# First layers' key and value compression over 128 rows and one weight slot, its operand built behind the last rotation

## What is computed

```python
blk_idx = CMP_STRIDE * jnp.arange(n_cmp)[:, None] + jnp.arange(CMP_BLOCK)[None, :]

def compress(t, p, w1, w2):
    tb = t[:, :, blk_idx] + p
    hid = jax.nn.gelu(tb.reshape(B, G, n_cmp, CMP_BLOCK * Dh) @ w1)
    return hid @ w2

kc = compress(partial_rope(kv[0, 0], pos), cmp_pos[0], cmp_w1[0], cmp_w2[0])
vc = compress(kv[0, 1], cmp_pos[1], cmp_w1[1], cmp_w2[1])
s_cmp = jnp.einsum('bghsd,bgnd->bghsn', q, kc)
```

## Time and profile before

| | |
|---|---|
| median of 3 runs | 1391.33 us (1391.18 to 1391.76) |
| profiled execution | 1391.72 us, of which the span of the trace is 1389.7 us |
| instructions | 31502 |
| PE busy | 1362.7 us, 98% |
| VectorE busy | 1052.0 us, 76% |
| ScalarE busy | 843.5 us, 61% |
| GpSimd busy | 553.1 us, 40% |
| granted TensorE clock, mean | 0.999 of full speed |

### The profile page before, as it was taken

One profiled execution on the slowest core, in us unless ns is written; L12 is line 12 of the kernel. 1 busy time (PEld: TensorE's weight loads), 2 busy tenths in 40 slices (PEclk: granted clock), 3 DMA queues, 4 the chain that ended last, 5 costly groups with the idle time before them and its releaser, 6 DMA issues.

```text
span 1389.7 us, 31502 instructions
## 1 busy us (share of the span) xinstructions
PE 1362.7 (98%) x13386; PEld 1168.5 (84%) x13386; DVE 1052.0 (76%) x1395; ACT 843.5 (61%) x1349; POOL 553.1 (40%) x448
## 2 busy tenths in 40 slices
PE   8999999999999999999999999999999999999997
PEld 7778888888778888888778888888888778988887
DVE  6897886557897884568888898756978865898853
ACT  5684554337675544346896755645788888675652
POOL 0144995122056992224210576603114212366610
PEclk9999999999999999999999999999999999999999
DMA  9543466544343666535335365553643333476551
GB/s 364 185 147 128 170 211 208 198 167 152 123 142 107 239 213 206 189 107 167 122 122 212 143 224 183 176 188 119 213 152 122 100 130 126 150 245 211 194 170 32
DMA packets 37020, 234.65 MB, mean 169 GB/s; under 512 B 4752, under 2 KB 7824, under 8 KB 10384
## 3 DMA queue, kind: packets, MB, share of 16 engines
q1 hardware_dynamic: 36880, 232.63, 48.8%
HBM read 231.57 MB, written 1.05 MB: 167 GB/s over the span
## 4 chain that ended last, share of the span: by engine, by line
PE 76%; DVE 12%; ACT 7%; issue 3%; POOL 1%; DMA 1%; ACTq 0%; DVEq 0%; SPq 0%; POOLq 0%
PE psum L734 22%; PE psum L736 21%; PE psum L735 21%; DVE low L2428 4%; ACT high L1734 2%; PE psum L819 1%; PE psum L820 1%; PE psum L821 1%; ACT m L2136 1%; PE psum L944 1%; DMA raw<-stream 1%; PE psum L940 1%; POOL h L3258 1%; POOL m L3256 1%; DVE arena L2535 1%
## 5 line engine op out<-in xcount | busy, mean ns | idle before, releaser
L2428 DVE SCALAR_TENSOR_TENSOR low<-raw,high 128x2048 f16<-128x2048 f32 (+5 forms) x247 | 533.1, 2165 | 186.1 <-ACT high L1734 185.4
L734 PE MATMUL psum<-u,high 128*128 128x256 f16 (+2 forms) x2008 | 552.7, 275 | 1.3 <-ACT arena L1720 1.3
L736 PE MATMUL psum<-u,low 128*128 128x256 f16 (+2 forms) x2008 | 552.4, 275 | 0.0
L735 PE MATMUL psum<-u,high 128*128 128x256 f16 (+2 forms) x2008 | 552.4, 275 | 0.0
L1734 ACT ACTIVATE high<-raw 128x2048 f16<-128x2048 f32 (+4 forms) x248 | 418.1, 1690 | 122.3 <-PE psum L736 88.6
L734 PE MATMUL psum<-arena,high 128*128 128x256 f16 (+2 forms) x1112 | 304.7, 274 | 1.7 <-DVE arena L2962 1.4
L736 PE MATMUL psum<-arena,low 128*128 128x256 f16 (+2 forms) x1112 | 304.7, 274 | 0.0
L735 PE MATMUL psum<-arena,high 128*128 128x256 f16 (+2 forms) x1112 | 304.7, 274 | 0.0
L734 PEld LDWEIGHTS psum<-u,high 128*128 128x128 f16 x2008 | 196.5, 98 | 34.2 <-issue 5.3
L735 PEld LDWEIGHTS psum<-u,high 128*128 128x128 f16 x2008 | 196.7, 98 | 28.8 <-issue 0.7
L736 PEld LDWEIGHTS psum<-u,low 128*128 128x128 f16 x2008 | 196.6, 98 | 28.1
(11 more groups left out here) (364 smaller groups left out, 1817.7 us busy)
## 6 DMA issues: line engine op xcount, KB each, us to landing
raw<-stream SPq DMA_DIRECT2D x206, 1024.0 KB, 4.8
raw<-stream SPq DMA_DIRECT2D x8, 768.0 KB, 4.2
raw<-stream SPq DMA_DIRECT2D x5, 512.0 KB, 3.6
raw<-stream SPq DMA_DIRECT2D x2, 896.0 KB, 4.5
con<-consts SPq DMA_DIRECT2D x1, 1437.0 KB, 12.3
h<-x_t SPq DMA_DIRECT2D x2, 512.0 KB, 5.8
raw<-stream SPq DMA_DIRECT2D x2, 448.0 KB, 5.2
misc<-small SPq DMA_DIRECT2D x1, 512.0 KB, 14.5
```

What stands on the lines that cost most here:

```text
L734: pe.matmul(out, w_hi, x[0], start=start, stop=False)
L735: pe.matmul(out, w_hi, x[1], start=False, stop=False)
L736: return pe.matmul(out, w_lo, x[0], start=False, stop=stop)
L2428: tell(dve.scalar_tensor_tensor(low[:, at:at + w], raw[:, off:off + w], W_SCALE, high[:, at:at + w], ALU.mult, ALU.subtract), split_ready ...
```

## The change

- The two weight slots of the compression per layer become one, `cmp_l`, of 2048 columns. Row r of the slot holds position parity and feature: window position 2i on rows 0 to 63 and 2i + 1 on rows 64 to 127. For each i, 64 columns are for keys and 64 for values. Slots behind it move up by one.
- `compressed_hidden` becomes one block: for each of 16 i, one matmul of 120 columns with the high weights (high and low operand, each 4 x 15) and one of 60 with the low weights, on all 128 rows. Keys times value windows and the reverse are computed too and not read. Keys' hidden values now lie on rows 0 to 63 and the values' on 64 to 127, and the scaling, sum and `compressed_keys` follow that.
- On PE the block stands where `compressed_hidden(0)` stood; where `compressed_hidden(1)` stood comes `one(T_PU + 1)`, which was between `turn(2)` and `compressed_keys`.
- On VectorE the two additions of `tb` behind `rotate(0)` go, and eight (key or value, head, parity) on 64 rows come behind `rotate(2)`, ahead of `give(6)`. `tb_lo` moves behind the four copies.
- On ScalarE `tb_hi` moves behind the evacuation of T_VS, ahead of `give(7)`; `compression(0)` and one of the two further low parts on VectorE go; `evac(T_PU + 1)` moves ahead; four small copies of kc and vc become two.

```diff
-        items.append(("product", f"in1_{l}", KT, [len(t) for t in nsa_gla_pool_order()], ((CMP_AFTER, f"cmp_{l}_0"), (CMP_AFTER, f"cmp_{l}_1"))))
+        items.append(("product", f"in1_{l}", KT, [len(t) for t in nsa_gla_pool_order()], ((CMP_AFTER, f"cmp_{l}"),)))
...
-                    for j in range(CMP_BLOCK):
-                        for g in range(2):
-                            r = slice(g * HD, g * HD + HD)
-
-                            at = (w1 % SPLIT) * SLOT + j * HD
-                            pe.matmul(shaped(bank(4 + g, 32 * which, 32 * which + 2 * CMP_N, r), 2, CMP_N), high[r, at:at + HD],
-                                      tb_parts[r, :, which, j, :], start=(j == 0), stop=False)
-                            mm = pe.matmul(bank(4 + g, 32 * which, 32 * which + CMP_N, r), low[r, at:at + HD], tb_hi[r, which, j, :],
-                                           start=False, stop=(j == CMP_BLOCK - 1))
+                    for i in range(CMP_BLOCK // 2):
+                        at = (w1 % SPLIT) * SLOT + i * P
+                        pe.matmul(shaped(bank(4, 0, 8 * CMP_N), 2, 4 * CMP_N), high[:, at:at + P], tb_parts[:, :, i, :], start=(i == 0), stop=False)
+                        mm = pe.matmul(bank(4, 0, 4 * CMP_N), low[:, at:at + P], tb_hi[:, i, :], start=False, stop=(i == CMP_BLOCK // 2 - 1))
                     mm.then_inc(slot_free, 1)
...
                 turn(0)
-                compressed_hidden(0)
+                compressed_hidden()
                 scores(2)
                 values(0)
                 turn(1)
-                compressed_hidden(1)
+                one(T_PU + 1)
                 scores(3)
                 values(1)
                 turn(2)
-                one(T_PU + 1)
                 compressed_keys()
...
-                act.wait_ge(tb_ready, 2 * l + 2)
-                tell(act.activation(tb_hi, tb, ACT.Copy), tb_high)
                 evac(T_Q + 1)
                 give(6)
                 evac(T_Q + 2)
                 evac(T_VS)
+                act.wait_ge(tb_ready, 2 * l + 2)
+                tell(act.activation(tb_hi, tb, ACT.Copy), tb_high)
                 give(7)
...
-                compression(0)
                 act.wait_ge(hid_summed, l + 1)
                 tell(act.activation(hid_tanh[:, :, 0:CMP_N], hid_tanh[:, :, 0:CMP_N], ACT.Tanh, scale=GELU_ROOT), hid_ready)
+                evac(T_PU + 1)
                 copy_out(1)
                 exps(3)
                 copy_pt(2)
-                evac(T_PU + 1)
...
                 rotate(0)
                 tell.settle()
-                evac_wait(T_VC)
-                for which, src in ((0, roped[:, T_KC, :]), (1, p1[:, T_VC, :])):
-                    windows = bass.AP(src.tensor, src.offset, [list(src.ap[0]), [1, CMP_BLOCK], [CMP_STRIDE, CMP_N]])
-                    pos = par[:, PAR[f"pos{l}"] + 32 * which:PAR[f"pos{l}"] + 32 * which + 32]
-                    tell(dve.tensor_tensor(tb[:, which], windows, along(pos, CMP_N), ALU.add), tb_ready)
                 give(4)
...
-                dve.wait_ge(tb_high, l + 1)
-                tell(dve.tensor_tensor(tb_lo, tb, tb_hi, ALU.subtract), tb_split)
                 dve.wait_ge(ds_done, l + 1)
...
                 rotate(2)
+                evac_wait(T_VC)
+                for which, src in ((0, roped[:, T_KC, :]), (1, p1[:, T_VC, :])):
+                    for g in range(2):
+                        r = slice(g * HD, g * HD + HD)
+                        rows = src[r, :]
+                        for odd in range(2):
+                            windows = bass.AP(rows.tensor, rows.offset + odd, [list(rows.ap[0]), [2, CMP_BLOCK // 2], [CMP_STRIDE, CMP_N]])
+                            at = PAR[f"pos{l}"] + CMP_BLOCK * which
+                            pos = par[r, at + odd:at + CMP_BLOCK:2]
+                            to = (2 * which + g) * CMP_N
+                            ins = dve.tensor_tensor(tb[odd * HD:odd * HD + HD, :, to:to + CMP_N], windows, along(pos, CMP_N), ALU.add)
+                    tell(ins, tb_ready)
                 give(6)
                 dve.wait_ge(o_done, l + 1)
                 for q in range(4):
                     dst, src = gla_out(gmix[:, 3:6, :], q)
                     ins = dve.tensor_copy(dst, src)
                 tell(ins, o_copied)
+                dve.wait_ge(tb_high, l + 1)
+                tell(dve.tensor_tensor(tb_lo, tb, tb_hi, ALU.subtract), tb_split)
                 maxima(0)
...
                 give(8)
                 weigh(3)
-                low_part(matrices[f"cmp_{l}_0"] + SPLIT)
                 maxima(4)
-                low_part(matrices[f"cmp_{l}_1"] + SPLIT)
+                low_part(matrices[f"cmp_{l}"] + SPLIT)
                 weigh(4)
```

More of the change, by code:

```diff
@@ L455, in two_stacks @@
          ep, en, qd, kinv, kend, kend_tok, gmix) = carve([
-             (N_IN1, S), (6, S), (6, S), (2, 32, 15), (2, 16), (16,), (2, HD), (4, P), (6, P), (2, 18), (12, 16), (5, 12),
+             (N_IN1, S), (6, S), (6, S), (CMP_BLOCK // 2, 4 * CMP_N), (2, 16), (16,), (2, HD), (4, P), (6, P), (2, 18), (12, 16), (5, 12),
              (2, 2, S), (2, 512), (12, P), (2, 16), (2 * S,), (2 * S,), (2 * S,),
@@ L480, in two_stacks @@
         tb_home = p1[:, T_GQ:T_GQ + 4, :].rearrange("p a b -> p (a b)")[:, 0:960]
-        tb_parts = shaped(tb_home.bitcast(F16), 2, 2, 32, 15)
-        tb_hi, tb_lo = halves(tb_home, 2, 32, 15)
+        tb_parts = shaped(tb_home.bitcast(F16), 2, CMP_BLOCK // 2, 4 * CMP_N)
+        tb_hi, tb_lo = halves(tb_home, CMP_BLOCK // 2, 4 * CMP_N)
         m_flat = m_all.rearrange("p k t -> p (k t)")
@@ L1140, in values_to_tokens, with compressed_hidden @@
                     mm.then_inc(v_turned, 1)
[L1142 removed]
+                def compressed_hidden():
                     pe.wait_ge(o_rstd, l + 1)
[L1144 removed]
+                    w1 = matrices[f"cmp_{l}"]
                     await_slot(w1)
                     pe.wait_ge(tb_split, l + 1)
[L1147 to L1155 removed]
+                    for i in range(CMP_BLOCK // 2):
+                        at = (w1 % SPLIT) * SLOT + i * P
+                        pe.matmul(shaped(bank(4, 0, 8 * CMP_N), 2, 4 * CMP_N), high[:, at:at + P], tb_parts[:, :, i, :], start=(i == 0), stop=False)
+                        mm = pe.matmul(bank(4, 0, 4 * CMP_N), low[:, at:at + P], tb_hi[:, i, :], start=False, stop=(i == CMP_BLOCK // 2 - 1))
                     mm.then_inc(slot_free, 1)
@@ L1160, in compressed_keys @@
                     for g in range(2):
-                        r = slice(g * HD, g * HD + HD)
-                        pe.matmul(bank(4 + g, 0, CMP_N, r), small_at(0, HD, r), hid[r, 0, 0:CMP_N], start=True, stop=True)
-                        mm = pe.matmul(bank(4 + g, 64, 64 + HD, slice(0, CMP_N)), hid[r, 1, 0:CMP_N], small_at(HD, 2 * HD, r),
+                        keys, values = slice(0, HD), slice(HD, P)
+                        pe.matmul(bank(4, 0, CMP_N, slice(g * HD, g * HD + HD)), small_at(0, HD, keys), hid[keys, g, 0:CMP_N], start=True, stop=True)
+                        mm = pe.matmul(bank(5, g * HD, g * HD + HD, slice(0, CMP_N)), hid[values, g, 0:CMP_N], small_at(HD, 2 * HD, values),
                                        start=True, stop=True)
@@ L1826, in give, with compression @@
                     high_part(steps[n][0] + SPLIT)
-                def compression(which):
-                    high_part(matrices[f"cmp_{l}_{which}"] + SPLIT)
+                def compression():
+                    high_part(matrices[f"cmp_{l}"] + SPLIT)
                 base = 6 * l
@@ L1935, in first_layer @@
                 copy_pt(2)
-                evac(T_PU + 1)
                 act.wait_ge(kcvc_done, l + 1)
[L1938 to L1942, removed]
+                act.activation(kc[:, 0:CMP_N], bank(4, 0, CMP_N), ACT.Copy, scale=0.5)
+                tell(act.activation(vc[0:CMP_N], shaped(bank(5, 0, P, slice(0, CMP_N)), 2, HD), ACT.Copy, scale=0.5), kcvc_ready)
                 copy_out(2)
-                compression(1)
+                compression()
                 exps(4)
@@ L2632, in first_layer @@
                 weigh(2)
-                freed_by_pe(dve, matrices[f"cmp_{l}_1"])
+                freed_by_pe(dve, matrices[f"cmp_{l}"])
                 h15, t15 = hid[:, :, 0:CMP_N], hid_tanh[:, :, 0:CMP_N]
[L2636 to L2639, removed]
+                for which in range(2):
+                    r, at = slice(which * HD, which * HD + HD), 2 * CMP_N * which
+                    high_sums = shaped(bank(4, at, at + 2 * CMP_N, r), 2, CMP_N)
+                    ins = dve.tensor_scalar(hid[r, :, 0:CMP_N], high_sums, 1.0 / W_SCALE, None, ALU.mult)
                 tell(ins)
                 tell.settle()
[L2642 to L2645, removed]
+                for which in range(2):
+                    r, at = slice(which * HD, which * HD + HD), 4 * CMP_N + 2 * CMP_N * which
+                    low_sums = shaped(bank(4, at, at + 2 * CMP_N, r), 2, CMP_N)
```

(6 more changed lines are left out.)

## The result

The changed kernel takes **1405.97 us** (median of 4 runs, 1404.39 to 1407.47) against 1391.32 of the kernel before on the same chip, a ratio of 1.0104 (95% interval 1.0088 to 1.0120). The sign and the main term were forecast. The size was not: 1397.7 was predicted, and the range ended at 1403.0. The profiled execution took 1406.91 us, of which the span is 1405.1; before it was 1391.72 and 1389.7.

What follows compares the result with a forecast made beforehand. VectorE was taken to have no room before `scores(0)`, PE only 0.3 us less. Delay +4.7 and gain −1.5 per layer made +6.4 over two: 1391.72 + 6.4 − 0.4 = 1397.7 us, range 1392.7 to 1399.7, or 1392.5 to 1403 with most of the clock case.

Steps and rivals of the forecast that it cites:

- main term: At `scores(0)`, PE stands still for copies delayed by the eight additions on VectorE: +4.7 us per layer (3.1 to 4.8).
- The build and its delay: Eight additions behind `rotate(2)` on VectorE, 0.58 us each, 4.6 in all, make the copies before `scores(0)` 4.7 us later per layer.
- Compression: On PE, 32 matmuls over 128 rows replace a block per layer, taking 1.5 us (1.3 to 1.76); PE loses 2.5 to 3.0.
- Rival 4: 120-column compression matmuls run slower than 0.055 us, up to 1.2 us more per layer: 1400; chance 0.51 together with the forecast.
- The gain: Compressed scores ready earlier at `compressed_turn(0)`: 0.6 to 2.4 us per layer, taken as 1.5.
- the shift: Behind `compressed_turn(0)` PE is continuous into out1, so the 1.5 us per layer gained there was to stay.
- The small new waits: PE waits at `scores(2)` (0.6 us not saved), a few tenths at compressed keys, and 1.0 to 1.3 idle before `scores(4)`.
- The sum without the clock: Whole kernel: +4.7 − 1.5 = +3.2 us per layer, +6.4 for two, giving 1397.7 us.
- rival 1: Clock falls in the new gap before `scores(0)`, costing 2.5 us per layer, +5 in all: 1402.7; chance 0.26.

Runs made afterwards that it cites:

- additions alone, gap filled: Kernel before plus the eight new additions behind the last rotation, result unread, and 38 idle matmuls in front of `scores(0)`: 1400.47 us, ratio 1.0065.
- old build, filled: Changed kernel with the two old additions back at their place and idle matmuls before `scores(2)`, compressed keys and `scores(4)`; compression computes other values: 1387.40 us, ratio 0.9969.
- all places filled: Changed kernel with idle matmuls before `scores(0)` (38) and in front of `scores(2)`, compressed keys and `scores(4)`: 1396.46 us.
- additions alone: Kernel before plus the eight new additions behind the last rotation, their result read by nobody: 1404.96 us, ratio 1.0093.
- old build: Changed kernel with the two old additions, `tb_hi` and `tb_lo` back at their old places, so the compression computes other values: 1391.7 us, ratio 1.0005.
- filling the gap alone: Changed kernel with 38 idle matmuls on PE between T_VW and `scores(0)`: 1398.7 us, ratio 1.0053.
- putting the pooled tile back alone: Changed kernel with T_PU + 1 back between `turn(2)` and the compressed keys, and its evacuation back too: 1400.8 us, ratio 1.0070.
- The run with the shorter gap: Changed kernel with the low part of `give(6)` moved from ahead of the four copies to behind `maxima(0)`: 1402.65 us, ratio 1.0073.
- split: Changed kernel with four additions ahead of `rotate(1)`, one in VectorE's wait, three behind `rotate(2)`, and `give(6)` behind `maxima(0)`: 1392.0 us, ratio 1.0005.

## Why the prediction was wrong

The parts, each from its own pair of runs, nearly add up (medians, each less its own kernel before):

| part | from | us, both layers |
|---|---|---|
| late copies | additions alone, gap filled, less before | +8.7 |
| rest of the change, clock held | old build, filled, less before | −4.3 |
| both, clock held | all places filled, less before | +4.7 |
| fall behind the gap | additions alone, less the same filled | +4.5 |
| fall in the light stretch | old build, less the same filled | +4.7 |
| all | 4.7 + 4.5 + 4.7 | +13.9 |

Measured were +14.6. The last 0.7 is within what the runs of one kernel with low stretches scatter (1404.4 to 1407.5). The first two rows make 4.4 where the third has 4.7. How the clock's 9.9 us are shared between the two places depends on which is mended first: in the changed kernel itself, filling the gap alone brings 7.3 us, and putting the pooled tile back alone brings 5.2.

- **The build and its delay: right.** 0.57 us per addition and 4.34 us of delay, against 0.58 and 4.7. Most of the difference is that the last rotation starts at 56.57 instead of 56.82, the 0.25 us that the prediction named and counted as nothing. The build itself took 4.55 us, where the 75 ns per instruction of the Trainium skill, "Vector Engine (DVE) Microarchitecture Reference", section 5.2, had made it 3.9. The row decides: additions that alternate between halves of the rows don't overlap.
- **Compression: right.** 32 matmuls in 1.3 us: a 120-column one is followed after about 0.05 us, and a pair takes 0.08. 1.5 was taken, with 1.3 as the sum's lower end. Rival 4 is out.
- **The gain: right in kind, small in size.** With the clock held it is 4.3 us, 2.1 per layer, where 1.5 was taken from 0.6 to 2.4. In that run (the old build, filled) `scores(4)` and `compressed_turn(0)` come 0.86 and 2.5 us earlier relative to `scores(0)`, about the most that was forecast (0.8 and 2.4). The prediction then had the shift stay; at the first matmul of the output product 2.0 us are left of the 2.5. GpSimd did not spoil the gain: L2686, the operation for which PE waited 1.7 us, took 1.41 before and takes 0.35 in the changed kernel, where pooling's last step is over before it starts. In the old build, filled, it is the same: 0.34 us at 93.54, with pooling over at 92.94. From the changed kernel (lines by shape, and GpSimd's timeline):

```profile
L2686 DVE TENSOR_TENSOR arena<-arena x2: 345/345/345, 102.8 to 410.9; 128x180 f32<-128x180 f32 x2
```

```profile
97.84 1.27 POOL L3285 TENSOR_TENSOR m<-m 128x512 f32<-128x512 f32 x1
```

- **The small new waits: right.** 0.70 us at `scores(2)`, where 0.6 of the saving was "not to be had"; 0.50 at the compressed keys ("a few tenths") and 0.69 at `scores(4)`, together 1.2, where the sum had 1.0 to 1.3 idle.
- **The sum without the clock: within its range.** 1396.5 against 1397.7: the change costs 4.7 us where 6.4 was summed, mostly because the gain was taken too small.
- **The step that failed: the clock, rival 1.** The sum had the clock at 1.00 everywhere, and the clock cost 9.9 us. The first place was described exactly, and the price of 2.5 us per layer was near 2.25, measured in the kernel with the additions alone; some luck is in that, since it was half of 4.9 us by choice, and in the changed kernel filling the gap brought 3.7 per layer, with a part of the second fall in it. Two things were wrong. First, it got a chance of 0.26, on the ground that "no gap of this length with work behind it is in the trace", while the earlier trace rows had already shown that 4.7 us or less is enough. The row that was there should have outweighed the row that wasn't, and rival 1 should have been the forecast. The run with the shorter gap says that even 2.46 us is enough, whereas the 1.69 at `compressed_turn(0)` before was not. Second, rival 1 took the clock as something that only a gap does, in one place. Nothing in it priced what `one(T_PU + 1)`, 24 matmuls of 256 columns in 2.6 us, does by standing in the middle of small products. With it gone, what lies between `scores(3)` and `scores(4)` are small matmuls, many on 64 rows and some of 15 or 64 columns, with waits of 0.5 and 0.7 us between, and the clock falls there. That costs 4.7 us, a little more than the 4.3 that the whole rest of the change gains. With rival 1 in both places the sum would have been 1397.7 + 5 + 4.7 = 1407.4.

The Trainium skill, "TensorE: Matmul & The Clock Gate", section "A second HAM failure mode: psum-queue depth-cycling", describes a kernel whose clock swings because PE idles in small pieces between groups of matmuls. The second place looks like it, with waits of 0.50 and 0.69 us between small products, but no run here shows that it is the same. The short waits by themselves don't decide: with T_PU + 1 at its old place PE waited longer in sum (5.4 us against 3.8 in these places), and the clock held.

## What to carry to other kernels

When PE's work is taken out or moved, look at what is left around that point as well as at the chain of waits: a block of large matmuls between small ones may be holding the clock for all of them. A gap or a light stretch that the change leaves on PE is to be priced at the lower clock for the work behind it, and a handful of idle matmuls can buy it back (10 here, 1.25 us in a place where PE waits, for some 4 us). And when a run has fewer instructions on PE and more busy time, compare the length of one and the same matmul in both traces before looking for anything else.

## What the runs showed of the hardware

- A wait of 2.46 us on PE, and one of 2.43 in layer two, was followed by 2.8 us and more at 1.2 GHz, beginning 0.4 us behind the wait's end in layer one and 0.9 in layer two; waits of 1.69 and 1.5 us were not. Between these nothing was measured.
- The clock fell without any wait over 0.7 us near it, in a stretch in which PE was busy most of the time (1.50 and 1.31 us of 2.00 from 84 and from 86 us in the changed kernel, and 10.20 of 10.20 once the clock was down). The low clock fills the waits up, so the busy share hides it; the granted clock and the length of one matmul show it.
- The low stretches of one kernel differ between its layers (3.3 us behind the gap in layer one, 6.6 in layer two) and, by the mean clock of each run, between executions: the old build took 1389.7 us at a mean clock of 0.997 and 1393.7 to 1394.1 at 0.992 to 0.993. This fits that the split and old builds scatter over 4.3 us, and the filled ones over 0.7 to 2.2 us.
- What was not tried: which property of the small matmuls (rows, columns, pauses between) lets the clock fall. The runs only show that 10 matmuls of 256 columns in their middle hold it.
